# Two transformer blocks on one core: weight and modulation loads interleaved in another order, and the backward-direction GLA factors and key copies moved

## The reference

```python
z = h @ w_in
u, vs, q, r, ga, gb, k, v, lr = _split(z, IN_SPLITS)
a = _spatial_gating(gelu(u), gelu(vs), sgu_ln_g, sgu_ln_b, sgu_w, sgu_b)   # layer norm over vs
o, s_f, s_b = _gla_bidir(qh, _heads(k), _heads(v), lr, gla_w2, gla_b2, s0f, s0b)
```

```python
b = jnp.cumsum(log_a, axis=2)
k_dec = k * jnp.exp(b_last - b)
q_dec = q * jnp.exp(b)
k_inv = k * jnp.exp(-b)
scores = jnp.where(mask, einsum(q_dec, k_inv), 0.0)
o_intra = einsum(scores, v);  state = exp(b_last) * state + einsum(k_dec, v)
```

## Time and profile before

| | |
|---|---|
| median of three runs | 1320.6 us |
| the profiled execution's own time | 1320.6 us |
| its span, first to last instruction | 1318.8 us |
| PE busy | 1290.7 us (98%) |
| PE weight loads | 1222.9 us (93%) |
| POOL busy | 875.5 us (66%) |
| DVE busy | 705.2 us (53%) |
| ACT busy | 702.6 us (53%) |
| moved by DMA | 217.75 MB, 165 GB/s on average |

### The profile page before, as it was taken

One profiled execution on the slowest core, in us unless ns is written; L12 is line 12 of the kernel. 1 busy time (PEld: TensorE's weight loads), 2 busy tenths in 40 slices (PEclk: granted clock), 3 DMA queues, 4 the chain that ended last, 5 costly groups with the idle time before them and its releaser, 6 DMA issues.

```text
span 1318.8 us, 28102 instructions
## 1 busy us (share of the span) xinstructions
PE 1290.7 (98%) x10039; PEld 1222.9 (93%) x10039; DVE 705.2 (53%) x1609; ACT 702.6 (53%) x1241; POOL 875.5 (66%) x383
## 2 busy tenths in 40 slices
PE   9999999999999999999999999999999999999996
PEld 3678899999999999998999989999999999999996
DVE  3989852323656551566355236555643776555623
ACT  3666553554555554475332237656665555666643
POOL 0447965687688879754223216888788787888794
PEclk9999999999999999989999899999999999999999
DMA  9985264455455556633112114555556554555562
GB/s 366 400 317 186 86 219 144 128 175 179 157 166 185 183 161 187 193 102 108 50 64 65 65 33 135 186 177 179 175 162 190 183 180 151 186 180 185 154 191 72
DMA packets 66022, 217.75 MB, mean 165 GB/s; under 512 B 9896, under 2 KB 17320, under 8 KB 62608
## 3 DMA queue, kind: packets, MB, share of 16 engines
q1 hardware_dynamic: 65936, 216.56, 50.5%
HBM read 215.48 MB, written 1.05 MB: 164 GB/s over the span
## 4 chain that ended last, share of the span: by engine, by line
issue 40%; POOL 36%; PE 21%; ACT 1%; DVE 1%; POOLq 1%; ACTq 0%; DVEq 0%
POOL w_lo L585 36%; PE bank L689 9%; PE bank L973 5%; PE bank L742 5%; POOL w_lo L592 1%; ACT h L1504 0%; POOLq L582 0%; POOLq L584 0%; ACT w_hi L1504 0%; PE bank L627 0%; PE bank L786 0%; PE bank L628 0%; PE bank L632 0%; PE bank L955 0%; PE bank L1009 0%
## 5 line engine op out<-in xcount | busy, mean ns | idle before, releaser
L585 POOL TENSOR_TENSOR w_lo<-w_raw,w_hi 128x1024 fp32r<-128x1024 f32 x340 | 813.5, 2405 | 402.1 <-ACT w_hi L1504 401.7
L1504 ACT ACTIVATE w_hi<-w_raw 128x1024 fp32r<-128x1024 f32 (+1 forms) x372 | 377.7, 1020 | 144.2 <-PE bank L742 50.0
L689 PE MATMUL bank<-a_hi,w_hi 128*128 128x256 f32 (+4 forms) x1032 | 293.4, 284 | 1.0 <-POOL w_lo L585 1.0
L689 PE MATMUL bank<-a_hi,w_lo 128*128 128x256 f32 (+4 forms) x1032 | 293.0, 284 | 0.0
L689 PE MATMUL bank<-a_lo,w_hi 128*128 128x256 f32 (+4 forms) x1032 | 292.8, 284 | 0.0
L666 PE MATMUL bank<-a_hi,w_hi 128*128 128x256 f32 (+2 forms) x720 | 211.5, 294 | 0.9 <-ACTq L1761 0.8
L666 PE MATMUL bank<-a_hi,w_lo 128*128 128x256 f32 (+2 forms) x720 | 208.4, 290 | 0.0
L666 PE MATMUL bank<-a_lo,w_hi 128*128 128x256 f32 (+2 forms) x720 | 208.3, 289 | 0.0
L689 PEld LDWEIGHTS bank<-a_hi,w_hi 128*128 128x128 f32 x1032 | 195.8, 190 | 1.5 <-POOL w_lo L585 1.2
L689 PEld LDWEIGHTS bank<-a_lo,w_hi 128*128 128x128 f32 x1032 | 195.8, 190 | 0.1
L689 PEld LDWEIGHTS bank<-a_hi,w_lo 128*128 128x128 f32 x1032 | 195.9, 190 | 0.0
(11 more groups left out here) (462 smaller groups left out, 2529.7 us busy)
## 6 DMA issues: line engine op xcount, KB each, us to landing
w_raw<-in_s SPq DMA_DIRECT2D x284, 512.0 KB, 3.5
w_raw<-in_down SPq DMA_DIRECT2D x48, 512.0 KB, 3.6
adaw<-in_w_ada SPq DMA_DIRECT2D x16, 1024.0 KB, 10.4
w_raw<-in_down SPq DMA_DIRECT2D x24, 384.0 KB, 3.2
adab<-in_w_ada_first SPq DMA_DIRECT2D x8, 1024.0 KB, 8.9
ctxt<-in_ctx SPq DMA_DIRECT2D x1, 1024.0 KB, 11.5
x<-in_x SPq DMA_DIRECT2D x1, 1024.0 KB, 15.4
out_h<-h SPq DMA_DIRECT2D x4, 256.0 KB, 2.7
```

The lines of the kernel that those rows point to most:

```text
L585: pool.tensor_tensor(w_lo[:, s], w_raw[:, s], w_hi[:, s].bitcast(F32), ALU.subtract) \
L689: ins = mm(banks[bank][:, tk], w_[:, s, k], x_[:, k, tk], start=(m == 0), stop=(m == 3 * KD - 1))
L1504: return nc.scalar.activation(out_, in_, f, **kw)
```

## The change

Three lists of calls are put in another order; no instruction is added or dropped but one register of the loop bookkeeping.

SP: pairs 8, 9 and 10 of the modulation rows are issued earlier among units 8 to 11. DVE: `queries_keys(1)` moves behind `differences(1)`, the memset of the second score buffer moves ahead of it, and the two helpers become one function. ACT: `keys(1, (0, 1))` moves behind the layer norm's square roots.

```diff
                     ada_rows(7)
-                    slot_units(8, 10)
                     ada_rows(8)
+                    slot_units(8, 9)
+                    ada_rows(9)
+                    slot_units(9, 10)
+                    ada_rows(10)
                     slot_units(10, 12)
-                    for p in range(9, 12):
-                        ada_rows(p)
+                    ada_rows(11)
                     slot_units(12, 16)
@@
             context_state(0)
-            keys(1, (0, 1))
             act.wait_ge(vs_var, 2)
             for n in range(2):
                 fn(mv[:, n, 2:3], mv[:, n, 1:2], ACT.Sqrt, bias=eps6[:, 0:1]).then_inc(vs_std, 1)
             nc.scalar.preload_act_table(ACT.Gelu)
+            keys(1, (0, 1))
             units("w_u", evac_u, 0, 1)
@@
             def queries_keys(d):
-                dve.wait_ge(exps_ready, 4 * d + 1)
+                e = (1, 2, 3) if d == 0 else (5, 6, 7)
+                dve.wait_ge(exps_ready, e[0])
                 v.tensor_tensor(qd[d][:], q1[:], qd[d][:], ALU.mult).then_inc(qk_ready, 1)
-                dve.wait_ge(exps_ready, 4 * d + 2)
+                dve.wait_ge(exps_ready, e[1])
                 v.tensor_tensor(ki[d][:], k1[:, :, 0:N1], ki[d][:], ALU.mult).then_inc(qk_ready, 1)
-
-            def chunk_factors(d):
-                dve.wait_ge(exps_ready, 4 * d + 3)
+                dve.wait_ge(exps_ready, e[2])
@@
             queries_keys(0)
-            chunk_factors(0)
             decayed_keys(0)
             modulations(15, 16)
-            queries_keys(1)
             scores(0)
             differences(1)
             dve.wait_ge(banks_free, out_of("w_v"))
-            dve.wait_ge(qk_ready, 3)
-            chunk_factors(1)
+            link(v.memset(sc_full[1], 0.0))
+            queries_keys(1)
             decayed_keys(1)
-            link(v.memset(sc_full[1], 0.0))
             second_state(0)
```

## The result

Five executions of the changed kernel took 1327.8 us in the median (1327.07 to 1332.47), five of the kernel before on the same chip 1320.58 us (1317.58 to 1320.94). The ratio is 1.007, with a 95% interval of 1.0049 to 1.0093: slower, by 7.2 us between the medians. The forecast was 1327.4 us. The profiled execution took 1328.4 us for a span of 1326.6; PE is busy 1291.4 us of it, as before.

The account below looks back on a forecast made before the run. PE's stream was taken to bound the kernel, busy 98% of the span. 1320.6 + 3.6 (loads) + 3.2 (late keys through DVE and ACT) = 1327.4 us, range 1322.5 to 1332.0.

Parts of the forecast that it names:

- Part 1, the loads: Start of w_v: units 10 and 11 land behind two more pairs, so w_v begins at 84.5, costing 3.6 us.
- The idle share of the queue: DMA queue between 66 and 73 us: 0.5 us idle gets filled, reducing the 5.0 us delay of unit 10.
- Part 2, VectorE: Products of d = 1, 3.45 us, leave a hole and delay the keys: `ks_ready` at 162.5 against 158.05.
- K: Time at which DVE finishes `ks` (`ks_ready`): 162.5 taken, bounds 156.2 and 165.1, against 158.05 before.
- one wait more: DVE beside POOL's blocks of units 24 to 27: one further wait of a block, raising 161.3 to 162.5.
- Part 3, ScalarE with part 2: Key copies behind the square roots wait for DVE's late `ks`; w_u tile 1 starts 3.2 us late, bounds 0 and 5.8.
- Alone it would cost next to nothing: ACT's new order without late keys: copies done near 166.5 and 167.0, just when PE asks at 166.65.
- The clock: Rival: PE's standstill before w_v drops its clock to 0.50, adding up to 3.4 us, 1330.8 us; chance 0.22.
- the 6.8 of the forecast: Whole slowdown without a clock fall: 3.6 us at w_v plus 3.2 us at the late keys; chance 0.45.
- Half of it: Rival: only the loads cost, 1324.2 us (chance 0.12), or only the DVE and ACT moves, 1323.8 us (0.10).
- Not slower: Rival: unit 10 lands by 74.9 or so, the 0.5 us wait before w_v goes, 1320.1 us; chance 0.07.
- three signs of being wrong: Unit 10 lands before 76, key copies stand ready when PE comes, or a later stretch gives time back.

Follow-up runs that it names:

- the second trace of the changed kernel: The unaltered changed kernel profiled again, on another chip beside a version with unread products before w_v; 1328.04 us against 1319.34 for the kernel before, ratio 1.0063.
- e8_w2s_later: Kernel before with one VectorE instruction, the remainder of the last w2 part, moved behind the next modulation pair; 1318.91 us against 1319.64, ratio 0.9994.

## Why the prediction was right, and where it was not

**Part 1, the loads: right.** Unit 10 was rounded at 78.76 (78.5 forecast), unit 11 at 80.02 (79.8), POOL ended at 84.59 (84.4), w_v began at 84.64 (84.5): 3.7 us for 3.6. That closeness is in part luck: in the six other traces with this order of loads unit 10 was rounded at 77.75 to 78.30, and w_v came 2.95 to 3.45 us later than in the kernel before. The idle share of the queue was filled, since the window went from 0.93 to 1.02, but unit 10 landed 4.8 us later than before, where two pairs are 5.0: only 0.2 of the 0.5 us came back.

**Part 2, VectorE: right in kind, mostly 0.4 to 0.7 us small.** K was taken as 162.5. Less what the stretch moved it came at 163.1 or 163.2 in three kernels, at 162.9 in three (in the changed one 169.02 - 6.1), and at 162.2 in the second trace of the changed kernel. The forecast had bounded how often DVE and POOL wait for each other and guessed one wait more; there was mostly a little more than that. The Trainium skill, SBUF — State Buffer, section "SBUF: two separate sides", describes an exclusive lock, by which the forecast's estimate had K at 163.2. By that rule, the traces agree three times, at 163.1 or 163.2; the other four lie below it, at 162.9 and 162.2. In the changed kernel `kd` and `ks` ran free, in 2.28 and 2.29 us for 3.38 and 3.24 in the earlier trace rows. Three others were held instead: the differences (3.19 us for 2.72), the first product (2.37 for 1.21) and, most of all, the two small products into `kmul` (2.35 for 0.37). In the kernel before:

```profile
142.29 2.72 DVE L2525 TENSOR_TENSOR kd<-ebuf 128x2048 f32<-128x2048 f32 x1
...
147.55 0.37 DVE L2559 TENSOR_TENSOR kmul<-kmul,dec 128x4 f32<-128x4 f32 x2
```

**Part 3, ScalarE with part 2: right, and so was the interplay.** From K to w_u tile 1 it was 7.8 us in both kernels (171.00 - 163.21 and 176.82 - 169.02), for the 8.1 of the forecast. So the cost is K - 159.6: 3.6 us for K = 163.2, and 3.5 measured (90.05 - 86.51). The forecast's 3.2 had K too small by 0.7 and the rest too large by 0.3. By the same reckoning the changed kernel lost 3.3 us here in its first trace and 2.6 in its second. "Alone it would cost next to nothing" held.

**The clock: taken for a rival, and it is what happened.** The sum's step that failed is the one that left the fall out, with 0.22 for it. Every kernel here whose PE waited 2.0 us or more for w_v (six of six) had it, and none that waited 0.5 us or less or was filled. Its price was overstated: "up to 3.4 us", while 6.8 us at 0.50 cost 2.4 to 2.9, measured up to the scores, since PE stood still in the first part of it, and 3.4 us cost 1.5 or 1.6. The Trainium skill, TensorE: Matmul & The Clock Gate, section "HAM oscillation — how this bites in real kernels", describes waits for DMA inside a matmul stream after which the engine runs at half clock. By that rule, which spoke against this change, the traces agree, and I gave it too little.

**The time.** The loads, the late keys and the fall come to 3.7 + 3.3 + 2.4 = 9.4 us in the first trace of the changed kernel and to 3.1 + 2.6 + 1.5 = 7.2 in the second. Between the medians it is 7.2 us in the first comparison and 8.7 in the second. So that the 6.8 of the forecast, which left the fall out, came within 0.4 us of the first figure was luck: the median of before was 1 us higher there than in the later comparisons, with more executions (1319.2 to 1319.6), and the late falls move a time by more than the fall at w_v does. Both medians of the changed kernel are inside the range. **Half of it** and **Not slower** are out: both halves cost, and unit 10 was rounded at 78.76, 3.9 us later than the 74.9 from which *Not slower* decides (2.85 us in the earliest of the other traces). Of the three signs of being wrong one came in part: a later stretch gave 1.6 us back, 0.6 of it a matter of the one trace of before.

What stays open: what decides whether a fall lasts 3.4 or 6.8 us at the same standstill (the changed kernel had both), why its keys were 0.7 us sooner in one trace than in the other, and why the late falls differ between executions. These move a single time by some 3 us, as much as a part of this change.

## What to carry to other kernels

On the full queue here, what was put ahead of a load delayed it by about its own transfer time (4.8 us for two pairs of 2.5). So before moving a transfer forward, name what is waiting behind it and how much slack that has: here next to none, against a delay of 5 us. The products of d = 1 filled a hole on VectorE and cost nothing there; at their new place, with the memset, they made the keys 4 to 5 us late, of which TensorE paid 1.7, so look at the hole before moving such work. A copy that frees a buffer belongs ahead of anything that waits for another engine: behind the square roots it cost nothing while the keys were early, and 1.6 us more once they were late. And a new standstill of the matmul stream can have a second price, in the clock behind it: every wait here of 2.0 us or more had it.

## What was not expected of the hardware

- A wait of 2.0 us of PE, with matmuls back to back on either side, was followed by 3.4 us at a granted clock of 0.50, at a cost of 1.6 us; the waits of 3.6 to 4.2 us by 3.4 or 6.8 us, at 1.5 to 2.9. Unread products in the standstill took the fall away in three kernels of three.
- The VectorE remainder of `w2`, with two inputs, and GpSimd's remainders of units 10 and 11 met in six kernels and held each other up: 1.6 or 1.7 and 3.4 us (DVE's, and POOL's of unit 11) in three of them, 2.8 and 3.4 or 3.2 and 3.3 in the two with one pair moved, and 3.9 and 2.4 in one. Apart, in `e8_w2s_later`, they took 1.22 and 2.4. The same program text can so have two timings, 0.5 us of wait at one place or 1.4 at another, and what decides between them is not shown.
